# Expert items one by one in a hybrid decoder step: gate/up ahead of the down product, and four weight buffers for all

## The chip, the cores and the metric

The kernel runs on one core of a Trainium2 chip. Its time is the device time of one execution in microseconds (us). TensorE is the matrix engine, VectorE, ScalarE and GpSimd are the others, and SyncE (SP) issues most of the DMAs. A DMA of any queue runs on the core's 16 DMA engines.

## What is computed

The reference is one inference step of a two-layer decoder trunk for 256 prompt rows and 32 sample rows (288 rows of 1024 floats). Layer one mixes rows by a chunked spatial gate, layer two by block-sparse attention. Behind each mixer stands the part that matters here, a mixture of 16 experts: every row picks one of four groups, and in it two of four experts.

```python
g_w, g_idx = lax.top_k(g_prob, 1)
e_w, e_idx = lax.top_k(e_prob, TOP_K_IN_GROUP)          # 2 of the 4 experts in the group
e_w = e_w / jnp.sum(e_w, axis=-1, keepdims=True) * g_w
expert = g_idx * EXPERTS_PER_GROUP + e_idx
gates = jnp.sum(jax.nn.one_hot(expert, N_EXPERTS) * e_w[..., None], axis=1)
a = jnp.einsum('nd,edf->nef', x, w_gate)                # 1024 -> 256 per expert
b = jnp.einsum('nd,edf->nef', x, w_up)
hid = jax.nn.silu(a) * b * gates[:, :, None]
y = jnp.einsum('nef,efd->nd', hid, w_down)              # 256 -> 1024
```

## The kernel before

The kernel doesn't compute every expert for every row. It makes a list of items: one item is one expert with up to 64 of its rows (64 slots, each row in two halves of 512, so 128 partitions). Items 0 to 15 are experts 0 to 15; an expert with more than 64 rows gets extra items behind them. Items are done in pairs, so `plan` writes the number of pairs, and a layer does 16, 18 or more items.

For each item these steps follow one another, each on its engine:

- VectorE makes a one-hot matrix of slots against rows (`one_hot`, L827), TensorE multiplies it with `marks` into a table (`table_of`, L1153), and VectorE turns the table into row indices, output indices and gates (`indices`, L845 to L854). One table serves a pair. Its results move through three stages (`shift`, L834 and L835).
- GpSimd copies the row index (`take`, L501) and issues an indirect DMA that gathers the item's rows from `h_rows` in HBM (L505).
- TensorE transposes the gathered rows (`rows_up`, L1162), and VectorE copies them to `x_slotsT` (`x_tile`, L875).
- TensorE does the gate and up products (L1182), 32 instructions, ScalarE the SiLU (L609), VectorE the product with up and gate (L895).
- TensorE transposes the hidden rows (L1193), VectorE copies them (L899), TensorE does the down product (L1200), 8 instructions, ScalarE copies it out (L612), and GpSimd scatters it to `y_rows` (L531).

In TensorE's queue the order for item q is: gate/up(q), the table of a later pair if q is even, `rows_up` of q+1, the hidden transposes of q, down(q). Nothing of q+1 but its transposes stands between gate/up(q) and down(q).

The weights of an item are 1 MB each for gate, up and down. There are four places for them: `ew_in`/`ew_down` 0 and 1, and `pre_in`/`pre_down` 0 and 1 in `half_a` and `half_b`. Items 0 to 3 are loaded before the layer's experts begin. SP's loop (`experts`, L378) then loads items 4 to 7 to the same places, each gate and up when gate/up of four items earlier is done, its down when that item's down is done; items 8 and up all go to `ew` 0 and 1 and wait for the item two before. SP's queue runs in order, waits included. After the last item SP waits for all scatters and loads the rows back (L411).

The line `hold` only waits; `AHEAD` are offsets of semaphores, so that a loop's waits are on positive values.

Of the kernel before, what the change touches and what calls it, by code (L numbers as in the profile page):

```python
# [27 lines left out]
def const_columns(T, TSA, TS):  # L28

    at, out = 0, {}  # L30
    for name, n in (("ident", P), ("keep_upper", P), ("causal_neg", P), ("cos", T), ("sin", T),
                    ("rotate", ROT), ("own_causal", TSA), ("own_neg", TSA * TSA // (GRP * TS)),
                    ("earlier", 16), ("later", 16), ("spread", TSA), ("before", P), ("limits", 4),
                    ("expert_tri", 256), ("expert_slot", 16), ("extra_slot", 16), ("extra_items", 10),
                    ("evens", 5), ("first_items", 16), ("lanes", 2 * P), ("halves", 2), ("marks", 18)):
        out[name] = slice(at, at + n)
        at += n
    return out, at
# [15 lines left out]
def hybrid_step(nc, t, o):  # L54
# [29 lines left out]
    with ExitStack() as ctx:  # L84
# [3 lines left out]
        def sem(name):  # L88
            return ctx.enter_context(nc.semaphore(name))
# [89 lines left out]
        marks = sb("marks", [P, NT, 2, 6], BF16)  # L179
        lanes = sb("lanes", [P, 2 * P], BF16)  # L180
        late = tri[0:1, 0:10 * NE].rearrange("p (i e) -> p i e", i=10)
        late_n = sb("late_n", [1, 10])
        pairs_f = sb("pairs_f", [1, 8])
        items = sb("items", [1, NE + 10], I32)
        pairs = sb("pairs", [1, 1], I32)
        table = sb("table", [P, 2, 6])
        tok_off = sb("tok_off", [P, 4])
        row_idx = sb("row_idx", [P, 2], I32)

        outs = sb("outs", [P, 3, 2], I32)  # L190
        slot_gates = sb("slot_gates", [P, 3, 2])
        out_idx = [sb(f"out_idx{u}", [P, 1], I32) for u in range(2)]
        in_idx = [sb(f"in_idx{u}", [P, 1], I32) for u in range(2)]
# [34 lines left out]
        hot = z_flat[:, 3712:3712 + 6 * P].bitcast(BF16).rearrange("p (c k n) -> p c k n", c=NT, k=2)  # L228
# [47 lines left out]
        E = [{n: sem(f"e{l}_{n}") for n in """step this slid taken planned xt xt_sb gu silued hid ht ht_sb dn y_sb hot tab idx out  # L276
              in0 in1 w0 w1 wd0 wd1 sc0 sc1""".split()} for l in range(DEPTH)]

        AHEAD = {"xt_sb": 2, "hid": 2, "ht_sb": 2, "y_sb": 2}
        s_pre = [sem(f"s_pre{u}") for u in range(2)]  # L280
        s_yb = [sem(f"s_yb{c}") for c in range(NT)]
# [5 lines left out]
        ISTEPS = 4  # L287
        Y_ORDER = [KT - 1] + list(range(KT - 1))
        QUADS = 2
# [31 lines left out]

        def upto(eng, s, n):

            if n > 0:
                eng.wait_ge(s, n)
# [5 lines left out]
        def _(sp):  # L331
# [41 lines left out]
            def prefetch(l, u):  # L373

                expert_in(l, 2 + u, pre_in[u], s_pre[u])
                expert_down(l, 2 + u, pre_down[u], s_pre[u])

            def experts(l):  # L378


                with sp.Fori(1, QUADS) as i:
                    for u in range(4):

                        w_in, w_down = (ew_in, ew_down) if u < 2 else (pre_in, pre_down)
                        hold(E[l]["gu"], 4 * i - 3 + u)
                        expert_in(l, 4 * i + u, w_in[u % 2], E[l][f"w{u}"] if u < 2 else s_pre[u % 2])
                        hold(E[l]["dn"], 4 * i - 3 + u)
                        expert_down(l, 4 * i + u, w_down[u % 2], E[l][f"wd{u}"] if u < 2 else s_pre[u % 2])

                def item(e, u, before):  # L390

                    hold(E[l]["gu"], before + 1)
                    expert_in(l, e, ew_in[u], E[l][f"w{u}"])
                    hold(E[l]["dn"], before + 1)
                    expert_down(l, e, ew_down[u], E[l][f"wd{u}"])

                for u in range(2):
                    item(4 * QUADS + u, u, 4 * QUADS - 4 + u)
                sp.wait_ge(E[l]["planned"], 1)
                n = sp.value_load(pairs[0:1, 0:1], min_val=NE // 2, max_val=NE // 2 + 5)  # L400
                with sp.Fori(2 * QUADS + 1, n) as i:
                    for u in range(2):
                        e = sp.value_load(items[0:1, bass.ds(2 * i + u, 1)], min_val=0, max_val=NE - 1)
                        item(e, u, 2 * i - 2 + u)
                for u in range(2):
                    hold(E[l][f"sc{u}"], 16 * n + 16)
                    hold(E[l][f"in{u}"], 16 * n + 16)
                hold(E[l]["xt_sb"], AHEAD["xt_sb"] + 2 * n + 1)
# [4 lines left out]
            for u in range(2):  # L413
                expert_in(0, u, ew_in[u], E[0][f"w{u}"])
                expert_down(0, u, ew_down[u], E[0][f"wd{u}"])
# [4 lines left out]
            prefetch(0, 1)  # L420
# [4 lines left out]
            prefetch(0, 0)  # L425
# [33 lines left out]
            prefetch(1, 0)  # L459
            for u in range(2):  # L460
                sp.wait_ge(S["pv"], 7 + u)
                expert_in(1, u, ew_in[u], E[1][f"w{u}"])
                expert_down(1, u, ew_down[u], E[1][f"wd{u}"])
            sp.wait_ge(S["proj"], 2 * KT)
            prefetch(1, 1)
# [12 lines left out]
        def _(pool):  # L478
            for l in range(DEPTH):
                for n, ahead in AHEAD.items():  # L480
                    pool.sem_inc(E[l][n], ahead)
# [6 lines left out]
            pool.tensor_copy(marks[:, :, :, 0:3], cst[:, cols["marks"]].rearrange("p (c k n) -> p c k n", c=NT, k=2)).then_inc(S["fill"], 1)  # L488
            pool.tensor_copy(items[:, 0:NE], cst[0:1, cols["first_items"]]).then_inc(S["fill"], 1)

            def experts(l):
# [7 lines left out]
                def take(u, done):  # L499

                    pool.tensor_copy(in_idx[u][:, :], row_idx[:, u:u + 1]).then_inc(E[l]["taken"], 1)  # L501
                    hold(E[l]["taken"], done)

                def gather(u):
                    pool.indirect_dma_start(out=x_slots[:, u, :], out_offset=None, in_=h_dram.rearrange("t (h n) -> (t h) n", h=2),  # L505
                                            in_offset=bass.IndirectOffsetOnAxis(ap=in_idx[u][:, 0:1], axis=0),
                                            bounds_check=2 * T - 1, oob_is_err=False).then_inc(E[l][f"in{u}"], 16)


# [5 lines left out]
                pool.wait_ge(E[l]["idx"], 1)  # L515
                for u in range(2):
                    take(u, u + 1)
                    gather(u)
                pool.wait_ge(E[l]["planned"], 1)
                n = pool.value_load(pairs[0:1, 0:1], min_val=NE // 2, max_val=NE // 2 + 5)  # L520
                with pool.Fori(0, n) as i:
                    hold(E[l]["idx"], i + 2)
                    for u in range(2):
                        hold(E[l][f"in{u}"], 16 * i + 16)
                        take(u, 2 * i + u + 3)
                        hold(E[l]["xt"], 2 * i + u + 1)
                        gather(u)
                    for u in range(2):
                        hold(E[l]["out"], 2 * i + u + 1)
                        hold(E[l]["y_sb"], AHEAD["y_sb"] + 2 * i + u + 1)  # L530
                        pool.indirect_dma_start(out=y_dram[l].rearrange("t k (h n) -> (t k h) n", h=2),  # L531
                                                out_offset=bass.IndirectOffsetOnAxis(ap=out_idx[u][:, 0:1], axis=0),
                                                in_=y_slots[:, u, :], in_offset=None,
# [1011 lines left out]
```

## Time and profile before

| | us |
|---|---|
| median of 3 runs (range) | 773.92 (772.51 to 776.78) |
| the profiled execution | 770.98 |
| its span, first to last instruction | 769.1 |
| TensorE busy (share of the span) | 628.2 (82%) |
| VectorE busy | 289.6 (38%) |
| ScalarE busy | 157.2 (20%) |
| GpSimd busy | 104.0 (14%) |
| mean granted TensorE clock | 0.914 |
| experts, layer one, first gate/up to end of last down | 186.05 to 311.36 |
| experts, layer two | 602.75 to 744.19 |

The two expert stretches are 267 us of the span. A busy share is a mean over stages with different limits; what an item costs is read from its stretch. Times in a timeline are from the span's start; "idle before" in brackets is how long the engine stood still ahead of the group and what it waited for. PE is TensorE, DVE VectorE, ACT ScalarE, POOL GpSimd.

### The profile page before, as it was taken

To read this page: it belongs to the slowest core of one execution; us is meant where nothing else is said; L and a number is where in the kernel's file an instruction comes from. 1 tells how busy PE (TensorE), PEld (TensorE's weight loads), DVE (VectorE), ACT (ScalarE), POOL (GpSimd) and SP (SyncE) were. 2 spreads that over 40 slices of the span, in tenths; PEclk is the share of its full clock that TensorE was granted. 3 is DMA by queue.
4 is the path that set the end of the run, shared out by engine and by line. 5 is a ranking of instruction groups with operands and counts; after the bars stand their busy time and mean duration, and the time that the engine had idled before them with its cause. 6 is when DMAs were issued, how large, how long until landed. Compare 5 with 4: busy or idle time off the path is not lost.

```text
span 769.1 us, 11977 instructions
## 1 busy us (share of the span) xinstructions
PE 628.2 (82%) x4067; PEld 430.0 (56%) x4067; DVE 289.6 (38%) x889; ACT 157.2 (20%) x326; POOL 104.0 (14%) x155
## 2 busy tenths in 40 slices
PE   5899999964899899279999997973987789898860
PEld 3677767732555555157667674662765456564430
DVE  2202121166334322244666775510027443334314
ACT  2115100020212221121112453211013113121210
POOL 0000000002222322000112000000000323322222
PEclk9999968995999999779999998995999799999995
DMA  9965030051997898599522774779923399699934
GB/s 343 290 266 219 22 150 1 0 212 37 381 410 296 330 412 354 173 386 319 170 95 95 237 245 144 244 222 360 404 80 148 131 401 411 239 406 414 409 138 174
DMA packets 65373, 187.82 MB, mean 244 GB/s; under 512 B 12044, under 2 KB 12606, under 8 KB 60982
## 3 DMA queue, kind: packets, MB, share of 16 engines
q1 hardware_dynamic: 58934, 175.50, 61.2%
q0 software_dynamic: 6400, 11.82, 4.2%
q8 instruction: 23, 0.38, 0.2%
q14 instruction: 16, 0.13, 0.1%
HBM read 182.95 MB, written 13.76 MB: 256 GB/s over the span
## 4 chain that ended last, share of the span: by engine, by line
PE 66%; DMA 10%; DVE 10%; SPq 5%; issue 5%; ACT 2%; DVEq 0%; POOLq 0%
PE PS L1097 26%; PE PS L1182 15%; PE PS L1200 7%; DMA ew_in<-in_moe_w_up 5%; PE PS L1088 3%; SPq L313 2%; SPq L311 2%; PE PS L1311 2%; DMA zT<-y_rows 2%; DMA half_b<-in_b_w_o 2%; PE PS L1268 2%; PE PS L1153 1%; PE PS L1113 1%; DVE zT L895 1%; PE PS L1265 1%
## 5 line engine op out<-in xcount | busy, mean ns | idle before, releaser
L1097 PE MATMUL PS<-hT,half_b 128*128 128x288 f32 x384 | 100.6, 422 | 10.4 <-DMA half_b<-in_b_w_o 7.1
L1182 PE MATMUL PS<-ew_in,zT 128*64 128x256 f32 x832 | 99.3, 392 | 6.3 <-DMA ew_in<-in_moe_w_up 3.1
L1097 PEld LDWEIGHTS PS<-hT,half_b 128*128 128x128 f32 x384 | 75.3, 197 | 34.4 <-issue 11.7
L1182 PEld LDWEIGHTS PS<-ew_in,zT 128*64 128x64 f32 x832 | 68.0, 142 | 45.3 <-issue 26.1
L895 DVE SCALAR_TENSOR_TENSOR zT<-PS,slot_gates,zT 64x256 f32<-64x256 f32 x34 | 16.5, 485 | 146.7 <-ACT zT L609 139.2
L1097 PE MATMUL PS<-hT,half_a 128*128 128x288 f32 x256 | 66.2, 417 | 3.1 <-DVE hT L725 3.1
L1200 PE MATMUL PS<-ew_down,zT 128*64 128x512 f32 x208 | 51.3, 611 | 14.5 <-issue 14.5
L1097 PEld LDWEIGHTS PS<-hT,half_a 128*128 128x128 f32 x256 | 49.0, 194 | 20.0 <-issue 4.1
L531 POOL DMA_INDIRECT y_rows<-zT,out_idx x34 | 34.3, 1010 | 149.4 <-ACT zT L612 149.4
L505 POOL DMA_INDIRECT zT<-h_rows,in_idx x38 | 39.8, 1046 | 50.3 <-PE PS L1162 18.7
L612 ACT COPY zT<-PS 128x512 f32<-128x512 f32 x34 | 19.9, 585 | 128.2 <-PE PS L1200 128.2
L511 POOL DMA_DIRECT2D h_rows<-tokbuf x2 | 1.7, 868 | 323.1 <-ACT tokbuf L600 323.1
L584 ACT ACTIVATE sq<-xT 128x288 f32<-128x288 f32 x32 | 13.6, 442 | 123.2 <-DVE xT L732 95.6
L578 ACT ACT_TABLE_LOAD x25 | 32.1, 1283 | 24.8 <-DVE pairs L867 23.7
L732 DVE TENSOR_TENSOR xT<-PS,xT 128x288 f32<-128x288 f32 x16 | 7.3, 458 | 70.5 <-PE PS L1097 70.5
L1097 PE MATMUL PS<-zT,half_a 128*128 128x288 f32 x128 | 33.4, 420 | 0.0
L1200 PEld LDWEIGHTS PS<-ew_down,zT 128*64 128x64 f32 x208 | 15.0, 137 | 30.7 <-issue 30.7
L723 DVE RECIPROCAL rec<-std 128x288 f32<-128x288 f32 x5 | 9.8, 1953 | 55.7 <-ACT std L588 55.7
L1162 PE MATMUL PS<-cst,zT 128*128 128x128 f32 x144 | 27.7, 316 | 3.1 <-DMA zT<-h_rows,in_idx 3.1
L609 ACT ACTIVATE zT<-PS 64x256 f32<-64x256 f32 x34 | 12.8, 377 | 83.1 <-PE PS L1182 83.1
L1097 PEld LDWEIGHTS PS<-zT,half_a 128*128 128x128 f32 x128 | 25.2, 198 | 7.2
L875 DVE COPY zT<-PS 128x512 f32<-128x512 f32 x36 | 24.9, 692 | 9.4 <-PE PS L1162 5.6
(258 smaller groups left out, 847.3 us busy)
## 6 DMA issues: line engine op xcount, KB each, us to landing
ew_in<-in_moe_w_gate SPq DMA_DIRECT2D x26, 1024.0 KB
ew_in<-in_moe_w_up SPq DMA_DIRECT2D x26, 1024.0 KB
ew_down<-in_moe_w_down SPq DMA_DIRECT2D x26, 1024.0 KB
ew_in<-in_cache_k SPq DMA_DIRECT2D x24, 256.0 KB, 4.8
ew_in<-in_cache_v SPq DMA_DIRECT2D x24, 256.0 KB, 3.4
half_a<-in_a_w_in SPq DMA_DIRECT2D x1, 4096.0 KB, 15.5
half_b<-in_a_w_in SPq DMA_DIRECT2D x1, 4096.0 KB, 25.8
half_a<-in_a_w_out SPq DMA_DIRECT2D x1, 4096.0 KB, 13.8
```

The source lines that it names most:

```text
L311: at = [eng.value_load(pages[0:1, bass.ds(b * NPAGE + j, 1)], min_val=0, max_val=NPOOL - 1) for j in pp]
L505: pool.indirect_dma_start(out=x_slots[:, u, :], out_offset=None, in_=h_dram.rearrange("t (h n) -> (t h) n", h=2), in_offset=bass.IndirectO ...
L531: pool.indirect_dma_start(out=y_dram[l].rearrange("t k (h n) -> (t k h) n", h=2), out_offset=bass.IndirectOffsetOnAxis(ap=out_idx[u][:, 0: ...
L578: act.activation(spare[:, :], eps[:, :], func)
L612: act.copy(y_slots[:, u, :], PS[:, 5 + u, :]).then_inc(E[l]["y_sb"], 1)
L875: dve.tensor_copy(x_slotsT[:, u], PS[:, u, :].rearrange("p (j h n) -> p j h n", j=4, h=2)).then_inc(el["xt_sb"], 1)
L895: dve.scalar_tensor_tensor(out=hid, in0=PS[SLOT:2 * SLOT, 2 + u, 0:EF], scalar=slot_gates[0:SLOT, 0, u:u + 1], in1=silu, op0=ALU.mult, op1 ...
L1088: mm = pe.matmul(PS[:, 7, 0:T], mean_d[:, :], sq[:, k, :], start=(k == 0), stop=(k == KT - 1))
L1097: mm = pe.matmul(PS[:, bank, 0:T], w[:, k, col:col + P], src[:, k, :], start=(k == 0), stop=(k == KT - 1))
L1162: mm = pe.transpose(PS[:, u, j * P:(j + 1) * P], x_slots[:, u, bass.ds(j, P, 4)], ident)
L1182: mm = pe.matmul(PS[f * SLOT:(f + 1) * SLOT, 2 + u, 0:EF], x_slotsT[:, u, k % 4, k // 4, :], w_in[u][:, f, k, :], start=(k == 0), stop=(k ...
L1200: mm = pe.matmul(PS[half * SLOT:(half + 1) * SLOT, 5 + u, :], hidT[:, f, :], w_down[u][:, f, half * HALF:(half + 1) * HALF], start=(f == 0 ...
```

## The change

- **Single items.** Items 0 to 14 are written out one by one, and item 15 and all extra items run in a loop. `plan` writes `n_more`, 1 + the number of extra items, in place of the number of pairs.
- **Order on TensorE.** For item q: gate/up(q), hidden transposes of q-1, table of q+3, `rows_up` of q+1, down(q-1). In the loop the order is gate/up(q), table of q+1, hidden transposes of q, `rows_up` of q+1, down(q).
- **Weights.** Items 0 to 14 all go round the four places, in the order `ew` 0, `pre` 1, `pre` 0, `ew` 1, and wait for the item four before. The down weights of `pre` have a semaphore of their own. Item 15 and the extra items all go to `ew` 1; an extra item's load waits for the item before it (`holds`).
- **Tables.** A table is for one item: 64 slots, each twice, 128 wide (`lanes`). `marks` has nine columns, three groups of three, so that one `tensor_reduce` over each group gives the row index, the output index and the gate (`found`), and one addition of `halves` gives both indices as integers (`where`). They lie in rings of 8; `shift`, `take` and the copies to `out_idx` are gone. The gather reads its index from the ring.
- In the loop VectorE makes the table of item q+1 ahead of the product of item q, and at the end of each turn waits for the scatter of item q (`sc1`) before it moves ring place 0 to place 7.

```diff
+            def expert(l, q, wait):
+                u = (0, 1, 0, 1)[q % 4]
+                streamed = q % 4 in (0, 3)
+                if wait:
+                    sp.wait_ge(E[l]["gu"], q - 3)
+                expert_in(l, q, (ew_in if streamed else pre_in)[u], E[l][f"w{u}"] if streamed else s_pre[u])
+                if wait:
+                    sp.wait_ge(E[l]["dn"], q - 3)
+                expert_down(l, q, (ew_down if streamed else pre_down)[u], E[l][f"wd{u}"] if streamed else s_pre_down[u])
             def experts(l):
+                for q in range(4, LAST):
+                    expert(l, q, True)
                 sp.wait_ge(E[l]["planned"], 1)
+                more = sp.value_load(n_more[0:1, 0:1], min_val=1, max_val=11)
+                with sp.Fori(0, more) as i:
+                    q = i + LAST
+                    e = sp.value_load(items[0:1, bass.ds(q, 1)], min_val=0, max_val=NE - 1)
+                    free = sp.value_load(holds[0:1, bass.ds(i, 1)], min_val=12, max_val=N_MAX - 1)
+                    hold(E[l]["gu"], free)
+                    expert_in(l, e, ew_in[1], E[l]["w1"])
+                    hold(E[l]["dn"], free)
+                    expert_down(l, e, ew_down[1], E[l]["wd1"])
...
+                for q in range(2):
+                    pool.wait_ge(E[l]["idx"], 2 * q + 2)
+                    gather(q, q, q)
+                for q in range(LAST):
+                    if q + 2 <= LAST:
+                        pool.wait_ge(E[l]["idx"], 2 * q + 6)
+                        pool.wait_ge(E[l]["xt"], q + 1)
+                        gather(q + 2, (q + 2) % RING, q % 2)
+                    if q >= 1:
+                        pool.wait_ge(E[l]["y_sb"], q)
+                        scatter(q - 1, (q - 1) % RING, (q - 1) % 2)
+                pool.wait_ge(E[l]["y_sb"], LAST)
+                scatter(LAST - 1, (LAST - 1) % RING, (LAST - 1) % 2)
                 pool.wait_ge(E[l]["planned"], 1)
+                more = pool.value_load(n_more[0:1, 0:1], min_val=1, max_val=11)
+                with pool.Fori(0, more) as i:
+                    q = i + LAST
+                    hold(E[l]["idx"], 2 * q + 4)
+                    hold(E[l]["xt"], q + 1)
+                    gather(q + 1, 0, 1)
+                    hold(E[l]["y_sb"], q + 1)
+                    scatter(q, LAST % RING, 1)
...
+                ready_for(ACT.Silu)
+                for q in range(LAST):
+                    gate(q)
+                    if q >= 1:
+                        out_rows(q - 1, scattered(q - 3)[1])
+                out_rows(LAST - 1, scattered(LAST - 3)[1])
+                more = act.value_load(n_more[0:1, 0:1], min_val=1, max_val=11)
+                with act.Fori(0, more) as i:
+                    q = i + LAST
+                    gate(q)
+                    out_rows(q, 16 * i + scattered(LAST - 2)[1])
...
+            def one_hot(l, q):
                 for c, (_, m) in enumerate(tok):
                     for k in range(2):
+                        last = dve.tensor_scalar(hot[0:m, c, k, :], lanes[0:m, :], slots[0:m, c, k:k + 1],
+                                                 -float(SLOT * q) if isinstance(q, int) else 0.0, ALU.subtract, ALU.is_equal)
                 last.then_inc(E[l]["hot"], 1)
+            def indices(l, q, r):
+                dve.wait_ge(E[l]["tab"], q + 1)
+                dve.tensor_reduce(found[:, r, :], PS[:, 7, 0:9].rearrange("p (a b) -> p a b", a=3), AX.X, ALU.add).then_inc(E[l]["idx"], 1)
+                dve.wait_ge(E[l]["idx"], 2 * q + 1)
+                dve.tensor_tensor(where[:, r, :], found[:, r, 0:2], halves, ALU.add).then_inc(E[l]["idx"], 1)
...
+                one_hot(l, 0)
+                for q in range(3):
+                    indices(l, q, q)
+                    one_hot(l, q + 1)
                 plan(l)
...
+                x_tile(0, 0)
+                for q in range(LAST):
+                    if q >= 1:
+                        gated_up(q - 1)
+                    gated(q, q % RING)
+                    x_tile(q + 1, q)
+                    if q + 3 <= LAST:
+                        if q >= 5:
+                            s, value = scattered(q - 5)
+                            dve.wait_ge(el[s], value)
+                        indices(l, q + 3, (q + 3) % RING)
+                        if q + 4 <= LAST:
+                            one_hot(l, q + 4)
+                gated_up(LAST - 1)
+                dve.tensor_scalar(slots[:, :, :], slots[:, :, :], -float(SLOT * NE), None, ALU.add).then_inc(el["slid"], 1)
+                dve.wait_ge(el["sc0"], scattered(8)[1])
+                more = dve.value_load(n_more[0:1, 0:1], min_val=1, max_val=11)
+                with dve.Fori(0, more) as i:
+                    q = i + LAST
+                    dve.wait_ge(el["slid"], i + 1)
+                    one_hot(l, q + 1)
+                    dve.wait_ge(el["hot"], q + 2)
+                    dve.tensor_scalar(slots[:, :, :], slots[:, :, :], -float(SLOT), None, ALU.add).then_inc(el["slid"], 1)
+                    indices(l, q + 1, 0)
+                    gated(q, LAST % RING)
+                    gated_up(q)
+                    x_tile(q + 1, q + 1)
+                    dve.wait_ge(el["sc1"], more_scattered(i))
+                    dve.wait_ge(el["idx"], 2 * q + 4)
+                    dve.tensor_copy(found[:, LAST % RING, :], found[:, 0, :])
+                    dve.tensor_copy(where[:, LAST % RING, :], where[:, 0, :]).then_inc(el["moved"], 1)
+                    dve.wait_ge(el["moved"], i + 1)
...
+                for q in range(3):
+                    table_of(q)
+                rows_up(0, gathered(0)[1], 0)
+                for q in range(LAST):
+                    gate_up(q, *tiles_in(q), q - 1)
+                    if q >= 1:
+                        gated_up(q - 1)
+                    if q + 3 <= LAST:
+                        table_of(q + 3)
+                    rows_up(q + 1, gathered(q + 1)[1], q)
+                    if q >= 1:
+                        down(q - 1, *tiles_down(q - 1), q - 2)
+                gated_up(LAST - 1)
+                down(LAST - 1, *tiles_down(LAST - 1), LAST - 2)
                 pe.wait_ge(el["planned"], 1)
+                more = pe.value_load(n_more[0:1, 0:1], min_val=1, max_val=11)
+                with pe.Fori(0, more) as i:
+                    q = i + LAST
+                    gate_up(q, ew_in[1], (el["w1"], 32 * i + 32 * (NE // 4)), q)
+                    table_of(q + 1)
+                    gated_up(q)
+                    rows_up(q + 1, 16 * i + gathered(LAST + 2)[1], q + 1)
+                    down(q, ew_down[1], (el["wd1"], 16 * i + 16 * (NE // 4)), q)
```

The lines taken out are those of the functions printed above.

## Rows read from the trace of the kernel before

**Rows 1.** The page, chain that ended last, shares by engine.

```profile
PE 66%; DMA 10%; DVE 10%; SPq 5%; issue 5%; ACT 2%; DVEq 0%; POOLq 0%
```

**Rows 2.** Timeline of PE, first items of layer one.

```profile
186.05 5.47 PE L1182 MATMUL PS<-ew_in,zT 128*64 128x256 f32 x32 [1.38 <-DVE zT L875]
...
195.60 3.65 PE L1182 MATMUL PS<-ew_in,zT 128*64 128x256 f32 x32
...
199.19 0.75 PE L1162 MATMUL PS<-cst,zT 128*128 128x128 f32 x4
...
200.33 0.42 PE L1193 MATMUL PS<-cst,zT 64*128 64x64 f32 x2 [0.40 <-DVE zT L895]
...
201.21 1.94 PE L1200 MATMUL PS<-ew_down,zT 128*64 128x512 f32 x8 [0.46 <-issue]
...
202.95 3.65 PE L1182 MATMUL PS<-half_a,zT 128*64 128x256 f32 x32
...
206.53 0.71 PE L1153 MATMUL PS<-marks,zT 128*128 128x6 bf16 x12
```

**Rows 3.** The same timeline, last down of layer one; item 0 and last down of layer two.

```profile
309.42 1.94 PE L1200 MATMUL PS<-ew_down,zT 128*64 128x512 f32 x8 [0.45 <-issue]
...
602.75 5.33 PE L1182 MATMUL PS<-ew_in,zT 128*64 128x256 f32 x32 [1.65 <-DVE zT L875]
...
742.24 1.94 PE L1200 MATMUL PS<-ew_down,zT 128*64 128x512 f32 x8 [0.46 <-issue]
```

**Rows 4.** Waits in layer two: who waited for whom, total us, times, longest.

```profile
ACT zT L612 <- PE PS L1200: 67.3, 18, 4.0
```

**Rows 5.** DMA queues of two stretches, 200 to 240 and 676 to 732 us: packets, MB, share.

```profile
q1 hardware_dynamic: 3277, 14.88, 92.6%
...
q1 hardware_dynamic: 4635, 21.33, 94.6%
```

**Rows 6.** Windows: busy time of each engine, granted clock, DMA share, GB/s.

```profile
244.00:246.00 2.00, 1.47 (x10) 0.87 (x6) 1.14 (x3) 0.38 (x1) 0.00 (x0) 1.00 0.36 135
...
252.00:254.00 2.00, 1.37 (x12) 1.07 (x13) 1.43 (x4) 0.10 (x1) 1.23 (x2) 1.00 0.46 80
...
660.00:662.00 2.00, 1.61 (x14) 0.89 (x11) 0.58 (x2) 0.38 (x1) 0.09 (x1) 1.00 0.73 297
...
670.00:672.00 2.00, 1.41 (x8) 0.67 (x10) 0.55 (x3) 0.00 (x0) 1.03 (x1) 1.00 0.86 317
```

**Rows 7.** Timeline of SP's queue, issue of item 10's first load.

```profile
251.94 0.41 SPq L333 DMA_DIRECT2D ew_in<-in_moe_w_gate  x1
```

**Rows 8.** The chain, in order of time: start, us, what.

```profile
282.76 12.90 DMA ew_in<-in_moe_w_up
...
699.93 12.23 DMA ew_in<-in_moe_w_up
```

**Rows 9.** Timeline of all engines ahead of item 0, layer one.

```profile
176.16 1.25 DVE L827 TENSOR_SCALAR zT<-lanes,slots 128x256 bf16<-128x256 bf16 x6
...
178.66 0.23 DVE L850 TENSOR_SCALAR row_idx<-tok_off,cst 128x2 int32<-128x2 f32 x1
...
180.22 1.11 POOL L505 DMA_INDIRECT zT<-h_rows,in_idx  x1 [0.96 <-POOL in_idx L501]
...
183.54 1.13 PE L1162 MATMUL PS<-cst,zT 128*128 128x128 f32 x4 [1.80 <-DMA zT<-h_rows,in_idx]
...
185.22 0.69 DVE L875 COPY zT<-PS 128x512 f32<-128x512 f32 x1 [0.95 <-PE PS L1162]
```

**Rows 10.** Landing times of the scatters of L531.

```profile
DMA to landing us min/median/max: 2.3/6.5/7.0
```

**Rows 11.** Timeline of PE in the attention.

```profile
470.02 1.11 PE L1311 MATMUL PS<-cst,half_a 128*128 128x128 f32 x4 [2.54 <-DVE half_a L970]
```

**Rows 12.** Windows around two gaps of PE (PEclk is the granted clock).

```profile
470.00:475.00 5.00, 3.95 (x16) 1.63 (x16) 1.17 (x4) 2.69 (x10) 0.00 (x0) 0.50 0.16 63
...
711.00:713.00 2.00, 0.50 (x6) 0.34 (x6) 1.54 (x9) 1.87 (x3) 0.43 (x1) 1.00 1.03 426
```

More of the change, by code:

```diff
@@ L411, in experts @@
                         load(dst[0:m, c, :], y_dram[l][at:at + m, k, :], s_yb[c])
[L413 to L415 removed]
+            expert(0, 0, False)
+            expert(0, 3, False)
             sp.wait_ge(S["z"], KT)
@@ L458, in _ @@
             sp.wait_ge(S["pv"], 6)
[L459 to L463, printed above, removed]
+            expert(1, 2, False)
+            sp.wait_ge(S["pv"], 7)
+            expert(1, 0, False)
+            sp.wait_ge(S["pv"], 8)
+            expert(1, 3, False)
             sp.wait_ge(S["proj"], 2 * KT)
-            prefetch(1, 1)
+            expert(1, 1, False)
             experts(1)
@@ L514, in experts @@
                     pool.wait_ge(E[l][f"sc{u}"], 16)
[L515 to L518, printed above, removed]
-                pool.wait_ge(E[l]["planned"], 1)
[L520 to L533, printed above, removed]
-                                                bounds_check=4 * T - 1, oob_is_err=False).then_inc(E[l][f"sc{u}"], 16)
@@ L1215, in experts, with gate_up @@
-                with pe.Fori(2 * QUADS, pairs_n) as i:
-                    pair(i, *streamed(i + 1 - QUADS))
+                def gate_up(q, w_in, landed_in, free):
+                    u = u_of(q)
+                    pe.wait_ge(*landed_in)
+                    pe.wait_ge(el["xt_sb"], q + 1)
+                    upto(pe, el["hid"], free)
+                    for k in range(KT):
+                        for f in range(2):
+                            mm = pe.matmul(PS[f * SLOT:(f + 1) * SLOT, 2 + u, 0:EF], x_slotsT[:, u, k % 4, k // 4, :],
+                                           w_in[:, f, k, :], start=(k == 0), stop=(k == KT - 1))
+                    mm.then_inc(el["gu"], 1)
@@ new lines, in gated_up, with down @@
+                def gated_up(q):
+                    pe.wait_ge(el["hid"], q + 1)
+                    upto(pe, el["ht_sb"], q)
+                    if not isinstance(q, int):
+                        pe.sem_inc(S["held"], 1)
+                    for f in range(FB):
+                        mm = pe.transpose(PS[:, 4, f * SLOT:(f + 1) * SLOT], hid[:, bass.ds(f, P, FB)], ident[0:SLOT, 0:SLOT])
+                    mm.then_inc(el["ht"], 1)
+                def down(q, w_down, landed_down, free):
+                    u = u_of(q)
+                    pe.wait_ge(*landed_down)
+                    pe.wait_ge(el["ht_sb"], q + 1)
+                    upto(pe, el["y_sb"], free)
+                    for f in range(FB):
+                        for half in range(2):
+                            mm = pe.matmul(PS[half * SLOT:(half + 1) * SLOT, 5 + u, :], hidT[:, f, :],
+                                           w_down[:, f, half * HALF:(half + 1) * HALF], start=(f == 0), stop=(f == FB - 1))
+                    mm.then_inc(el["dn"], 1)
```

288 lines of the change are left out of this document (103 added, 185 removed).

## The prediction

> **What bounds the kernel now.** I read the chain that ended last first, for which engine carries it: two thirds is TensorE, and a tenth is DMA [rows 1]. Then TensorE's timeline through the expert stretch of each layer, for the time of one item; then the DMA share in short windows, for when the weight stream stands still; last the waits, for how many items there are.
>
> An item on TensorE is gate/up 3.6 us, every second item a table 0.7 (half of it 0.35), the transposes of the next rows 0.7, hidden transposes 0.4, down 1.74 from its start to the next item [rows 2]. From 195.60 to the next item's start at 202.95 it is 7.35 us; with a table 7.7. Of this some 0.4 to 0.65 us twice an item is idle: TensorE waits for SiLU and product (ahead of L1193), then for the copy of the transposes (ahead of L1200). Item 0 starts at 186.05, the last product of the first layer ends at 309.42 + 1.94 = 311.36, of the second at 742.24 + 1.95 = 744.19 [rows 2, 3]. The second layer does 18 items [rows 4]; the two together 34, so the first does 16.
>
> The weight stream is the other limit. In its full stretches the hardware queue moves 14.88 MB in 40 us and 21.33 MB in 56 us [rows 5]: an item of 3.146 MB takes 8.46 or 8.26 us. I take 8.4, which is more than TensorE's 7.5. It is saved by the four items already there and paid back late: the stream stands still from about 244.7 to 253.5 (only 80 GB/s in the window to 254) and, in layer two, from 661.5 to 670 [rows 6], because items 10 and up may use only the two ew buffers (loads of item 10 are issued at 251.94 [rows 7], after item 8's gate/up). From there TensorE waits for weights: item 14's arrive at 295.66 and 712.16 [rows 8].
>
> **The prologue.** Before: one-hot starts 176.16, row index ready 178.89, copied by GpSimd, gather issued 180.22, rows transposed from 183.54, copied at 185.22, item 0 at 186.05 [rows 9]. After: six half-wide compares (0.2 us each as before, 1.05 in all; the trace has 1.25 for 256 wide), half a table 0.4, two VectorE instructions in place of three to reach an index, and no GpSimd copy: index 0 at about 178.0, gather issued about 179.1. But VectorE now makes three indices and four one-hots before item 0's copy: 177.2 + 3 x (0.4 + 0.45 + 1.05) = 182.9, plus a plan shorter by two instructions, 1.15: copy at 184.05, item 0 at 184.95. That is 1.1 us earlier; in layer two, where the first table waits for other transposes, 0.6. If the half-wide compare with two operations costs 0.3 instead of 0.18, this gain is gone (+2.3 us a layer); at its cheapest (0.15) it is 0.6 more.
>
> **Next item's gate/up ahead of the down product.** It adds no instruction: gate/up(q), hidden transposes(q-1), table, rows(q+1), down(q-1). SiLU and product lie under the down product, the copy of the transposes under table and rows, so both idle times go: 3.6 + 0.4 + 0.35 + 0.7 + 1.74 = 6.8 us an item, if VectorE and GpSimd keep up. GpSimd can: the two issues and their preparation are 3.9 us an item. But for the first ten items this gains nothing lasting, since the stream's 8.4 us bounds the end.
>
> **Four buffers for all.** SP's queue runs in order, and behind its wait for down(0) stand the loads of items 5 and on. down(0) comes after gate/up(1), at 184.95 + 5.5 + 0.3 + 0.7 + 1.0 (item 1 waits for its rows' copy here) + 3.6 + 0.4 + 1.0 + 1.94 = 199.4. Item 4's gate and up flow at 192.1 (issue plus 1.5, as around 251.94 [rows 6, 7]) and end at 197.7; the rest flows from 200.9: 3.2 us lost, against 8.8 gained. Then nothing stops it: every slot is free 6.8 us after the last. Item 14's gate/up weights are through 10.0 items later, 284.9. By the same sum item 14 of before would be there at 253.5 + 4.67 x 8.4 = 292.7 and 670 + 39.2 = 709.2; it came 3.0 later both times [rows 8], with other loads under way behind it. So 287.9, and 705.1 in layer two, where item 0 starts at 602.75 - 0.6 [rows 3].
>
> **The tail is where it is given back.** From item 14's weights on, TensorE does gate/up(14) 3.6, hidden(13) 0.4, rows(15) 0.7, down(13) 1.74, hidden(14) 0.4, the now bare copy 0.6, down(14) 1.74 = 9.2: item 15 starts at 297.1 and 714.3 (its own weights are there: 8.4 after item 14's). Reading the count is taken at nothing, under down(14); uncovered it costs 0.95 (the gap on VectorE before the copy at 185.22 [rows 9]).
> Items from 15 on are in the loop, where the table of item q+1 is made after gate/up(q), and the transposes of the rows of q+1 stand ahead of down(q) in TensorE's queue. So each such item holds a whole round trip: table 0.35, index 0.45, gather issued 0.95 later, landing 3.1 after the issue (180.22 to 183.54 [rows 9] is 3.3 at most), transposes 0.7, down 1.94: 7.5 us from the end of gate/up to the end of down, against 3.9 now. The layer ends at 297.1 + 3.65 + 7.5 = 308.2 with the clock held.
> Layer two has one extra item or two by its 18. I routed the given inputs by the reference: its fullest expert has 68 rows, one over 64, so one extra item, and 17 in place of 18. The saved empty item is worth its 7.5 us, but item 16 is serial: its weights wait for gate/up(15) (718.0), flow 719.5, arrive 724.7 to 725.5; and VectorE waits at the loop's end until the scatter of item 15 has landed before it makes the next one-hot. From down(15) (725.5): copy 0.6, scatter 0.9, landing 3.3 (2.3 at the least and 6.5 in the median [rows 10]; item 16's down weights flow just then), moves 0.5, one-hot 1.1, table 0.4, index 0.45, gather 1.1 + 3.0, transposes 0.7, down 1.94 = 14.0: end 739.5.
>
> **The clock.** TensorE idles about 3 us in each such round trip. Idle for 2.54 us ahead of 470.02 [rows 11], its granted clock was 0.50 from 470 to 475; around a gap of 1.5 us, 711 to 713, it stayed 1.00 [rows 12]. So I let it fall from 2.4 to 1.2 GHz after each: +1.5 us on down(15) in both layers, +2.0 on the last transposes and down. The Trainium skill, "TensorE: Matmul & The Clock Gate", Part 1, says that a gate halves the clock after an idle window; by it the rival below in which the clock holds is excluded, where the rows leave it open.
>
> **The sum.** Layer one 309.7 against 311.36: -1.6. Layer two 725.5 + 1.5 + 14.0 + 2.0 = 743.0 against 744.2: -1.2. Together -2.8 us on the profiled 770.98 (span 769.1); the median of the runs shown is 773.92, so 771.1.
>
> **Rivals.**
> *The clock holds* (the gaps are split by small transposes, as that of 1.5 us was): -1.6 - 1.5 and -1.2 - 3.5, together -7.8: 766.1. Against it stands the 470 row. Chance 0.25.
> *The stream gains more*: without the 3.0 us of late landing (less is queued at the end than now) both layers start item 15 up to 2.2 earlier: -2.8 - 4.4 = -7.2, 766.7. Against it: two rows show 3.0. Chance 0.13.
> *Slower: gathers and scatters land late.* If in the loop they take the 6.5 us of [rows 10] in place of 3.0 to 3.3, layer one pays 3.5, layer two 3.5 + 3.2 + 3.5: +13.7, so 784.8. It decides from 1.7 us more a trip (four trips, over 2.8 + 3.9). For it: stray loads behind; against it: the stream is nearly empty in all four. With half of it 778. Chance 0.2.
> The Trainium skill, "DMA: Bandwidth & Descriptors", section "Latency and other measured facts", gives 0.2 us for an HBM access on average and 2 us at high load; by it the four trips would cost at most 7.2 us more, an estimate of 775.6 with everything else as forecast.
> *It doesn't do what it says:* in the static part GpSimd issues gather(q+3) only after scatter(q-1), 3.5 us after down(q-1); landing may take 7.7 before TensorE waits. If it does, the item is 7.5 as now, still under 8.4: nothing changes but the first ten items. It is in the forecast's range.
>
> Forecast (clock falls, landings short) 0.42, its own range 768 to 775. The 80% range takes in the fast rivals (766) with the cheap bound of the compares and item 15 early (762), and half the slow landing: 762 to 779. Within 0.5% (3.9 us, about what this kernel's measurement can tell from no change) are most of the forecast and a little of the slow one, 0.38; faster the two fast rivals, 0.38; slower 0.24, the slow rival and the dear compares.
>
> **What would show it.** Right: DMA share 1.0 from about 201 to 297 with no gap; item 15's gate/up at 297 and 714; 7 to 9 us from its end to the end of down; 33 items; a granted clock of 0.5 in the round trips. Wrong: TensorE idle ahead of the row transposes in items 1 to 14 for more than 1.6 us an item, a stream that pauses again, or round trips of 10 us and more.

## The result and the profile after

The changed kernel takes 780.1 us (median of 4 runs, 779.1 to 782.5), the kernel before beside it 773.2 (772.3 to 776.8): a ratio of 1.008, 95% interval 1.005 to 1.011. It is slower by 0.8%; 771.1 was predicted. The profiled execution took 779.1, its span is 777.1 against 769.1, and its mean granted clock 0.89 against 0.914.

The page of the changed kernel: the chain that ended last, by engine, and the row transposes among its lines (L1194), which answer to [rows 1].

```profile
PE 64%; DMA 19%; DVE 9%; SPq 3%; issue 2%; ACT 2%; POOLq 0%; DVEq 0%; ACTq 0%
...
L1194 PE MATMUL PS<-cst,zT 128*128 128x128 f32 x140 | 28.1, 327 | 11.6 <-DMA zT<-h_rows,where 11.6
```

The share of DMA in the chain has doubled, and TensorE is idle for 11.6 us ahead of the transposes of gathered rows. The timeline of TensorE (start, duration, what, in brackets the idle time ahead of it and what ended it) through layer one, in answer to [rows 2, 3]:

```profile
184.52 6.13 PE L1205 MATMUL PS<-ew_in,zT 128*64 128x256 f32 x32 [1.18 <-DVE zT L885]
...
197.52 1.94 PE L1227 MATMUL PS<-ew_down,zT 128*64 128x512 f32 x8
199.28 3.62 PE L1205 MATMUL PS<-half_a,zT 128*64 128x256 f32 x32
...
205.99 3.62 PE L1205 MATMUL PS<-ew_in,zT 128*64 128x256 f32 x32
...
247.10 3.67 PE L1205 MATMUL PS<-half_b,zT 128*64 128x256 f32 x32 [0.75 <-DMA half_b<-in_moe_w_up]
...
290.11 3.67 PE L1205 MATMUL PS<-half_a,zT 128*64 128x256 f32 x32 [2.04 <-DMA half_a<-in_moe_w_up]
...
299.26 3.65 PE L1205 MATMUL PS<-ew_in,zT 128*64 128x256 f32 x32
302.84 0.39 PE L1184 MATMUL PS<-marks,zT 128*128 128x9 bf16 x6
304.30 0.42 PE L1216 MATMUL PS<-cst,zT 64*128 64x64 f32 x2 [1.07 <-DVE zT L890]
306.92 1.13 PE L1194 MATMUL PS<-cst,zT 128*128 128x128 f32 x4 [2.20 <-DMA zT<-h_rows,where]
307.98 3.68 PE L1227 MATMUL PS<-ew_down,zT 128*64 128x512 f32 x8
```

The period of an item is 6.7 us (199.28 to 205.99) until its weights are late, from item 9 on; then every gate/up up to item 14's waits for them. Items 9 to 14 start 8.60 us apart ((290.11 - 247.10) / 5). The last down product stands behind rows that nobody needs, runs at half clock (3.68 in place of 1.94) and ends at 311.66, where it ended at 311.36 before. What the stream had gained is gone within the last 9 us of the layer.

The same timeline at the end of layer two, from item 15's gate/up, with the instructions of other engines that its waits name:

```profile
719.42 3.67 PE L1205 MATMUL PS<-ew_in,zT 128*64 128x256 f32 x32
...
723.36 0.38 SPq L351 DMA_DIRECT2D ew_in<-in_moe_w_gate  x1
...
723.84 0.42 SPq L351 DMA_DIRECT2D ew_in<-in_moe_w_up  x1
...
724.87 1.04 POOL L508 DMA_INDIRECT zT<-h_rows,where  x1 [2.89 <-issue]
...
730.85 1.13 PE L1194 MATMUL PS<-cst,zT 128*128 128x128 f32 x4 [5.95 <-DMA zT<-h_rows,where]
731.91 3.68 PE L1227 MATMUL PS<-ew_down,zT 128*64 128x512 f32 x8
735.37 3.77 PE L1205 MATMUL PS<-ew_in,zT 128*64 128x256 f32 x32
...
741.01 0.17 DVE L932 COPY found<-found 128x3 f32<-128x3 f32 x1 [8.30 <-DMA y_rows<-zT,where]
...
742.88 0.41 PE L1184 MATMUL PS<-marks,zT 128*128 128x9 bf16 x6 [3.74 <-DVE zT L855]
...
747.97 3.68 PE L1227 MATMUL PS<-ew_down,zT 128*64 128x512 f32 x8
```

SP issues 2 MB of weights for item 16 at 723.36 and 723.84; the gather of item 16's rows is issued 1 us later and reaches TensorE at 730.85. Item 15's down product, whose operands have been there since 725.2, waits behind it. Layer two's experts end at 751.65; from the first gate/up (604.40) they take 147.3 us, 141.4 before. The waits from 600 us on (total, times, longest) count 17 items, so 33 with layer one's 16:

```profile
ACT zT L628 <- PE PS L1227: 66.0, 17, 12.1
```

Of the 8.0 us of span, 0.3 is layer one's end, 1.4 the attention and dense part between the layers, 5.8 layer two's experts, 0.5 what follows them.

### The profile page after: what moved, and what is told of

The parts are those of the page before. It is cut to its first block, busy times and chain, and to the rows that moved or that the text cites. A ratio compares the mean times of both kernels' runs of the same rounds, so it can differ in the third digit from the quotient of the medians.

```text
span 777.1 us, 10893 instructions
## 1 busy us (share of the span) xinstructions
PE 628.2 (81%) x3979; PEld 417.1 (54%) x3979; DVE 277.4 (36%) x794; ACT 134.1 (17%) x294; POOL 92.1 (12%) x114
## 4 chain that ended last, share of the span: by engine, by line
PE 64%; DMA 19%; DVE 9%; SPq 3%; issue 2%; ACT 2%; POOLq 0%; DVEq 0%; ACTq 0%
PE PS L1128 25%; DMA half_a<-in_moe_w_up 12%; PE PS L1205 10%; PE PS L1227 6%; PE PS L1360 3%; PE PS L1119 3%; PE PS L1194 2%; DMA zT<-y_rows 2%; DMA half_b<-in_b_w_o 2%; SPq L351 2%; PE PS L1317 2%; PE PS L1377 2%; PE PS L1144 1%; DMA zT<-h_rows,where 1%; PE PS L1184 1%
## 5 line engine op out<-in xcount | busy, mean ns | idle before, releaser
L1128 PEld LDWEIGHTS PS<-hT,half_b 128*128 128x128 f32 x384 | 75.5, 198 | 34.3 <-issue 11.6
L1205 PE MATMUL PS<-ew_in,zT 128*64 128x256 f32 x544 | 67.0, 402 | 9.2 <-DMA ew_in<-in_moe_w_up 6.3
L1205 PEld LDWEIGHTS PS<-ew_in,zT 128*64 128x64 f32 x544 | 42.2, 146 | 39.2 <-issue 14.1
L896 DVE COPY zT<-PS 128x128 f32<-128x128 f32 x33 | 9.6, 292 | 134.7 <-PE PS L1216 111.9
L513 POOL DMA_INDIRECT y_rows<-zT,where x33 | 33.5, 1014 | 179.0 <-ACT zT L628 174.2
L508 POOL DMA_INDIRECT zT<-h_rows,where x35 | 35.9, 1026 | 59.7 <-DVE where L865 34.2
L1227 PE MATMUL PS<-ew_down,zT 128*64 128x512 f32 x136 | 38.2, 687 | 0.0
L855 DVE TENSOR_SCALAR zT<-lanes,slots 128x128 bf16<-128x128 bf16 (+1 forms) x210 | 37.0, 247 | 1.7 <-DVE slots L917 1.2
L1194 PE MATMUL PS<-cst,zT 128*128 128x128 f32 x140 | 28.1, 327 | 11.6 <-DMA zT<-h_rows,where 11.6
L1205 PE MATMUL PS<-half_a,zT 128*64 128x256 f32 x256 | 29.2, 381 | 9.0 <-DMA half_a<-in_moe_w_up 9.0
L1205 PE MATMUL PS<-half_b,zT 128*64 128x256 f32 x256 | 29.3, 381 | 5.8 <-DMA half_b<-in_moe_w_up 4.0
L1205 PEld LDWEIGHTS PS<-half_a,zT 128*64 128x64 f32 x256 | 18.0, 137 | 22.9 <-DMA half_a<-in_moe_w_up 12.5
```

Source lines behind the costliest of these rows:

```text
L855: last = dve.tensor_scalar(hot[0:m, c, k, :], lanes[0:m, :], slots[0:m, c, k:k + 1], -float(SLOT * q) if isinstance(q, int) else 0.0, ALU. ...
L1128: mm = pe.matmul(PS[:, bank, 0:T], w[:, k, col:col + P], src[:, k, :], start=(k == 0), stop=(k == KT - 1))
L1194: mm = pe.transpose(PS[:, u, j * P:(j + 1) * P], x_slots[:, u, bass.ds(j, P, 4)], ident)
L1205: mm = pe.matmul(PS[f * SLOT:(f + 1) * SLOT, 2 + u, 0:EF], x_slotsT[:, u, k % 4, k // 4, :], w_in[:, f, k, :], start=(k == 0), stop=(k == ...
L1227: mm = pe.matmul(PS[half * SLOT:(half + 1) * SLOT, 5 + u, :], hidT[:, f, :], w_down[:, f, half * HALF:(half + 1) * HALF], start=(f == 0), ...
```

## The experiments

Twelve measurements were made in three groups, each group on one chip with the kernel before: 775.9 us there in the first (19 runs), 773.9 in the second (24), 775.1 in the third (29). Single executions of one kernel lie up to 1.2% apart, so the ratios decide, and differences inside a group.

**Down product ahead of the next rows, in the loop.** TensorE's queue in the loop, both layers:

```
-    rows_up(q + 1, ...)
     down(q, ...)
+    rows_up(q + 1, ...)
```

> The changed kernel with two lines swapped in TensorE's loop for items 15 and up: the down product ahead of the transposes of the next rows. Theory A (the tail's round trip is the loss: the down product stands behind a gather): layer one's last down product ends near 307 us instead of 311.7, layer two's near 741 instead of 751.7, because item 15's down product, its scatter and the copy behind it come 8 us sooner; about 765 to 769 us, faster than the kernel before. Rival B (the tail is bound by the single weight buffer, and the gather only fills that wait): item 16's gate/up starts within 1 us of where it does now, 735.4, and the whole is within 4 us of the changed kernel, 776 to 780.

Measured: 769.3 us (8 runs), 0.992 of the kernel before (0.989 to 0.995). TensorE in layer two:

```profile
725.37 3.62 PE L1227 MATMUL PS<-ew_down,zT 128*64 128x512 f32 x8 [0.43 <-issue]
731.00 0.75 PE L1194 MATMUL PS<-cst,zT 128*128 128x128 f32 x4 [2.01 <-DMA zT<-h_rows,where]
732.60 5.14 PE L1205 MATMUL PS<-ew_in,zT 128*64 128x256 f32 x32 [0.86 <-DVE zT L885]
...
739.99 1.94 PE L1227 MATMUL PS<-ew_down,zT 128*64 128x512 f32 x8 [0.43 <-issue]
```

The rows of item 16 still come at 731.0, but down(15) is done by then and its scatter has nearly landed, so the table of the next item needs no wait (VectorE idles 1.93 us ahead of its moves in place of 8.30). Item 15's gate/up to the last down's end is 22.5 us in place of 32.2. Layer one's last down ends at 307.9. Two lines in another order turn 0.8% slower into 0.8% faster.

**The buffer part alone.** The kernel before, its four buffers used for three turns in place of two:

```
-        QUADS = 2
+        QUADS = 3
```

> The kernel before with one number changed, QUADS from 2 to 3: items 0 to 11 go round four weight buffers instead of 0 to 7, all else as it was. It is the buffer part of the change alone. Theory (the stream's standstill of 8 to 9 us a layer is what makes items 12 and up wait): the standstill moves behind item 13's weights, TensorE no longer waits for weights in layer one, whose last down product ends near 308.5 instead of 311.4, and waits less in layer two; 768 to 771 us, 3 to 5 us faster than before. Rival (the stream's total decides and the standstill only moves): within 1.5 us of before.

Measured: 768.1 us (6 runs), 0.989 (0.985 to 0.992). Layer one's experts end at 308.0 in its profile, and TensorE waits for no weights in either layer. With the second measurement below (767.7 against 773.9), the third turn of the buffers alone is worth 6 to 8 us.

**Item 16's weights only after item 16's rows.** SP's issue is held on the gather:

```
     hold(E[l]["gu"], free)
+    hold(E[l]["in1"], 32 * i + gathered(LAST - 2)[1])
```

> The changed kernel with one more wait in SP's loop: item 16's weights are issued only when the gathered rows of item 16 have landed. It tells why that gather took 5.9 us longer than its partner in layer one. Theory (it queues behind 2 MB of item 16's own weights): TensorE waits about 2.2 us for it instead of 5.95, item 15's down product ends near 732 instead of 735.6, item 16's weights come near 735, so the end hardly moves (within 2 us). Rival (the gather is slow by itself, by its addresses or by the table): the wait stays near 6 us and the whole is 4 us longer.

One execution, 777.3 us. The timeline:

```profile
724.44 1.04 POOL L509 DMA_INDIRECT zT<-h_rows,where  x1 [2.84 <-issue]
...
727.19 1.13 PE L1195 MATMUL PS<-cst,zT 128*128 128x128 f32 x4 [2.72 <-DMA zT<-h_rows,where]
727.38 0.38 SPq L351 DMA_DIRECT2D ew_in<-in_moe_w_gate  x1
...
735.03 1.40 PE L1206 MATMUL PS<-ew_in,zT 128*64 128x256 f32 x8 [3.10 <-DMA ew_in<-in_moe_w_up]
```

With the weights out of the way the rows are there 2.75 us after the gather's issue; behind 2 MB of weights it was 5.98 (724.87 to 730.85). So the gather was late because item 16's weights were under way. Gate/up of item 16 gains nothing (735.03, now waiting 3.1 us for its weights), but item 15's down product and its scatter come earlier, so the last down product still ends sooner, 30.1 us after item 15's start in place of 32.2:

```profile
745.40 3.68 PE L1228 MATMUL PS<-ew_down,zT 128*64 128x512 f32 x8
```

What that is worth in the whole, one execution does not tell.

**The old order for items 0 to 14.** gate/up, table, rows, hidden transposes and down of one item, with VectorE's order to match; the rest of the change stays:

```
-    gate_up(q); gated_up(q - 1); table_of(q + 3); rows_up(q + 1); down(q - 1)
+    gate_up(q); table_of(q + 3); rows_up(q + 1); gated_up(q); down(q)
```

> The changed kernel with items 0 to 14 in the old order on TensorE: gate/up, table, next rows, hidden transposes, down of the same item; VectorE's order follows. Theory A (the weight stream bounds the layer, so running gate/up ahead is worth nothing, and it delays the first down product and with it the stream): items take 7.5 us until the stream catches up, item 4's down weights are issued 3 us sooner, and item 15 starts 1 to 4 us sooner than 299.3; 774 to 780 us. Rival B (running ahead is what keeps TensorE off the path): item 15 starts 3 us or more later, 783 us or more.

Measured: 775.3 us (12 runs), 0.9994 (0.997 to 1.002), although the one profiled execution, at 780.1 its slowest, starts item 15 of layer one at 299.2 as the changed kernel does. By that profile I had read that running ahead is worth nothing. The interval says something else, so it ran again below.

**Down first in one layer.** The edit of the first experiment, in layer one alone, then in layer two alone:

> The changed kernel with down(q) ahead of the transposes of rows(q+1) in layer one alone. In the runs so far layer one's experts ended between 307.9 and 311.7 us, yet the projection that waits for w_o's DMA in the middle started at 535.4 to 537.3 in all but one. Theory (the middle swallows what layer one's experts gain: its projections start earlier but at the lower clock, and then it waits for cache and w_o weights): last down product of layer one ends at 307.9 in place of 311.7, the w_o projection still starts at 536 to 537, and the whole is within 2 us of the changed kernel (778 to 780). Rival (layer one's gain passes through): 3.7 us earlier everywhere behind, 776.

> The same edit in layer two alone. Theory: nearly all of what the edit brought in both layers together (769.3 against 780) comes from here, since nothing behind layer two swallows it: item 15's and item 16's down products no longer stand behind late rows; end of the last down product 7.5 to 9 us earlier than in the changed kernel for the same start, time 770 to 773. Rival (both layers carry equal parts): 775.

> The changed kernel itself, on the same chip as the three beside it, as the base that they are compared with. Theory: 778 to 781, 0.8% over the kernel before. If the 0.8% were a matter of one chip or of how the clock happened to fall, it would be within 0.5% here.

Layer one alone: 776.4 us (12 runs), 1.0027 (1.0005 to 1.0048). Layer two alone: 773.1 (12 runs), 0.9987 (0.9966 to 1.0008). The changed kernel beside them: 779.2 (7 runs), 1.008 (1.005 to 1.011). So by the medians layer one brings 2.8 us and layer two 6.1; by the ratios 4.1 and 7.2, and the intervals allow either. Layer one's experts end 3.5 us earlier than in the first profile of the changed kernel (308.2 against 311.7). My theory that the middle swallows layer one's gain fell: the projection that I expected to start at 536 to 537 started at 534.1, and most of the gain, if not all, comes out at the end.

> The kernel before with QUADS = 3 once more, beside the others: it takes only the third turn of the four buffers and leaves the order of pairs. Theory: 0.988 to 0.992 of the kernel before (765 to 769), level with or a little under the changed kernel with down first in both layers, and clearly under down first in layer two alone, if layer one counts at all; as fast as that one if it does not.

Measured: 767.7 us (6 runs), 0.992 (0.989 to 0.995), as expected.

**Running ahead, measured beside its base.** Four kernels on one chip: the old order again, both edits together, down first alone, the changed kernel.

> The changed kernel with the old order of an item for items 0 to 14, again, now beside the changed kernel on one chip. It had 0.9994 of the kernel before where the changed kernel has 1.008, although in its one profiled execution, its slowest, item 15 of layer one started at the same 299.2 us. Theory (running ahead costs, through the clock or through extra requests that collide, not through the order of the tail): ratio to before 0.998 to 1.002 again, 4 to 7 us under the changed kernel beside it. Rival (the two came from different chips, and running ahead is worth nothing): within 2 us of the changed kernel beside it, 777 to 781.

> Both edits: down(q) ahead of the next rows in the loop, and the old order for items 0 to 14. Theory (running ahead costs 4 to 7 us by itself): 763 to 766, the fastest of all. Rival (worth nothing): the same as down first alone within 2 us, 768 to 770.

> Down first in both layers, as the base of the run with both edits. Both theories: 0.990 to 0.995 of the kernel before, 9 to 12 us under the changed kernel beside it.

> The changed kernel, as the base of the other three on this chip. Both theories: 1.005 to 1.011 of the kernel before.

| | median us (runs) | ratio to before |
|---|---|---|
| the change | 780.1 (12) | 1.0066 (1.004 to 1.009) |
| old order of items | 774.3 (12) | 0.9998 (0.997 to 1.003) |
| down first | 770.0 (12) | 0.9925 (0.990 to 0.995) |
| both | 763.3 (6) | 0.985 (0.981 to 0.989) |

Running ahead costs 5.7 us by itself and 6.7 where down goes first. Both edits together, which keep the four buffers, the single extra items and the short tables, are the fastest version, 1.5% under the kernel before. A part of why it costs shows in SP's queue. First the changed kernel, then the old order (start of item 0: 184.52 and 186.55):

```profile
190.68 0.37 SPq L351 DMA_DIRECT2D ew_in<-in_moe_w_gate  x1
191.09 0.47 SPq L351 DMA_DIRECT2D ew_in<-in_moe_w_up  x1
199.49 0.34 SPq L351 DMA_DIRECT2D ew_down<-in_moe_w_down  x1
```

```profile
192.03 0.37 SPq L351 DMA_DIRECT2D ew_in<-in_moe_w_gate  x1
192.44 0.47 SPq L351 DMA_DIRECT2D ew_in<-in_moe_w_up  x1
196.05 0.34 SPq L351 DMA_DIRECT2D ew_down<-in_moe_w_down  x1
```

Item 4's down weights wait for down(0). Run ahead, down(0) stands behind a whole gate/up, and 8.4 us pass between the issues of up and down weights in place of 3.6: the stream has run dry meanwhile (a DMA share of 0.03 from 198 to 200 us, 1.03 in the old order). TensorE's waits in layer two, 600 to 720 us, first of the changed kernel on this chip:

```profile
PE PS L1205 <- DMA half_a<-in_moe_w_up: 4.9, 2, 3.0
PE PS L1205 <- DMA ew_in<-in_moe_w_up: 3.3, 2, 1.7
...
PE PS L1205 <- DMA half_b<-in_moe_w_up: 1.6, 1, 1.6
```

and all those of the old order that are over 1 us:

```profile
PE PS L1225 <- issue: 7.5, 13, 0.6
PE PS L1203 <- DVE zT L885: 1.6, 1, 1.6
PE PS L1182 <- DVE zT L855: 1.5, 1, 1.5
PE PS L1225 <- DVE zT L896: 1.3, 2, 0.6
```

In the old order TensorE waits for no weights at all, although item 14's have to be there only 0.8 us later (711.52 against 710.74). And when the stream does bind, running ahead is the worse place to be caught: from item 14's gate/up to item 15's are 9.28 us (710.74 to 720.02: two down products lie between), in the old order 7.34 (711.52 to 718.86). From the start of layer two's item 0 to item 15's gate/up it is 114.8 us run ahead and 113.6 in the old order; from 116.3 to 113.4 with down first.

So these rows account for 1.2 and 2.9 us in layer two. But about 1.6 of the 2.9 is the clock: in that profile of down first, item 14's gate/up ran at half clock for a part, behind its wait for weights, and item 15's starts 10.83 us after it in place of the 9.28 above:

```profile
706.99 5.36 PE L1205 MATMUL PS<-half_a,zT 128*64 128x256 f32 x32 [1.97 <-DMA half_a<-in_moe_w_up]
```

In six of the eight profiles of kernels that run ahead, one to four gate/up products behind such a wait took 5.36 us in place of 3.67; the three profiles of the old order have no such wait and no such product. So running ahead has a second price, which differs from one execution to the next. How much of it reaches the end is not shown.

In layer one the same stretch is 1.7 shorter (113.0 against 114.7), but item 0 starts 2.0 later there in all three profiles of the old order, since the first gather comes 5.1 us after its issue in place of 3.3; why, stays open. The profiled execution of the old order was, at 778.4, again 4 us over its median, so how the 5.7 us add up in a typical execution stays open too.

## Why the prediction was wrong, by its steps

The forecast of the span was 766.3; it is 777.1. Two steps failed by what they assumed, that running ahead "gains nothing lasting" (put at nothing, measured at 5.7 to 6.7 us lost) and that the stream is nearly empty in every round trip (one trip of 9.0 us took 12.5); the time of the weight stream was mis-sized besides, by 5.0 us in the two layers. The 10.8 us between forecast and profile, step by step:

- **Prologue: right.** Item 0 of layer one starts at 184.52, forecast 184.95. The six half-wide compares take 1.05, and GpSimd copies nothing.
- **6.8 us an item run ahead: right**, 6.7. That it "gains nothing lasting" was the trap: I priced it at nothing for items 0 to 9, and it costs. I had its two prices in the text, the 3.2 us in which the stream stands still at item 4 and the 9.2 from item 14's weights to item 15's start, and compared neither with the old order, where they are nothing and 7.35.
- **Item 14's weights at 287.9 and 705.1: wrong by 2.2 and 5.2.** The item was put at 8.4 us of stream, between 8.46 and 8.26 [rows 5]; it is 8.60 here (above). Ten items at 0.2 are 2.0 us a layer. From item 0's start, items 15 began 2.6 and 2.9 late; with item 0 of layer one 0.4 early, that is 2.2 and 2.9: 5.0 us. What the other 0.6 to 0.9 a layer is, was not followed.
- **Layer one's round trip and fallen clock: right.** Gate/up's end to down's end, 7.5 + 1.5 forecast, is 8.8 (302.9 to 311.66), with the last down at half clock. The windows of the changed kernel show the granted clock of 304 to 310 and 731 to 735, in answer to [rows 12]:

```profile
304.00:310.00 6.00, 3.50 (x12) 1.80 (x14) 1.13 (x3) 0.00 (x0) 1.04 (x1) 0.63 0.02 3
731.00:735.00 4.00, 4.00 (x12) 1.57 (x14) 0.69 (x1) 0.00 (x0) 0.00 (x0) 0.50 0.00 0
```

  The Trainium skill, "TensorE: Matmul & The Clock Gate", Part 1, has the clock halved after idling, and the trace agrees (0.50 in the second window, behind an idle time of 5.95 us). In all three profiles of the changed kernel the down products of the three trips ran at half clock, wholly or in part (2.86 to 3.68 us in place of 1.94). But that the rival in which the clock holds was excluded beforehand, as the prediction has it, goes too far: idle times of 2 us left the clock up in one execution of this kernel and halved it in another (last section).
- **Layer two's trip of item 15: the step that failed is "the stream is nearly empty in all four".** It is not in this one: SP issues item 16's weights on the same event, the end of gate/up(15), that starts the round trip, and 1 us ahead of its gather. The prediction has these weights in its own text ("flow 719.5, arrive 724.7 to 725.5") and did not set them beside the gather. The trip took 12.5 us in place of 9.0: 3.5 more. The rival of late landings had the mechanism and priced it at 3.2 to 3.5 in each of four trips; one had it. The estimate of 775.6 behind that rival is added up wrong (771.1 and 7.2 is 778.3), and it gives a trip 1.8 us more where this gather took 3.2 more (5.98 against 2.75).
- **The extra item: right.** From down(15)'s end to the last down's end, 14.0 + 2.0 forecast, 16.06 measured: the scatter landed 3.9 us after its issue (737.15 to 741.01), the gather came 2.2 after.
- **The middle: not priced, 2.0 us.** The forecast moved layer one's gain through unchanged. In these two profiles TensorE's clock came back later after the change. The mean squares and first projection of layer two, before:

```profile
329.86 5.73 PE L1088 MATMUL PS<-sq,mean_d 128*128 128x288 f32 x16 [0.64 <-ACT sq L584]
338.88 9.69 PE L1097 MATMUL PS<-hT,half_b 128*128 128x288 f32 x32 [3.29 <-DVE hT L725]
```

and after:

```profile
330.11 7.19 PE L1119 MATMUL PS<-sq,mean_d 128*128 128x288 f32 x16 [0.64 <-ACT sq L595]
340.59 10.94 PE L1128 MATMUL PS<-hT,half_b 128*128 128x288 f32 x32 [3.29 <-DVE hT L753]
```

  That is 2.7 us in two groups of instructions that are the same in both kernels. The granted clock was 0.50 from 322 to 333 us in both; from there to 337 it was 0.99 before, and after the change still 0.50 until 335. But nothing shows that the change does this. A second profile of the changed kernel, whose last down product ran at half clock too, has the short times:

```profile
332.45 5.65 PE L1119 MATMUL PS<-sq,mean_d 128*128 128x288 f32 x16 [0.64 <-ACT sq L595]
341.39 9.69 PE L1128 MATMUL PS<-hT,half_b 128*128 128x288 f32 x32 [3.29 <-DVE hT L753]
```

  And the kernel before with three turns of its buffers took the long ones in one profile (7.11 and 10.89), with its last down product at full clock, and the short ones in the other. From the last down of layer one to item 0 of layer two, the changed kernel takes 292.7, 290.3 and 293.5 us in its three profiles, and the kernel before 291.4 in its one. So this term is as large as what it differs by from one execution to the next.
- **After the experts**: 0.5 us more (25.4 against 24.9).

The terms 2.16 + 2.87 + 3.47 + 1.95 + 0.54, less the 0.14 by which layer one's trip and layer two's tail together beat the forecast, are 10.85. Against the kernel before, which is what the ratio measures, the experiments weigh the parts: down behind the next rows +10.1 us (780.1 to 770.0; +11.1 in the old order, 774.3 to 763.3), running ahead +5.7 to +6.7, the rest of the change -11.8 (763.3 against 775.1). Of that rest the third turn of the buffers brings 6 to 8 us by itself; the single items, the short tables and the item saved in layer two were not measured one by one. I had named the transposes "ahead of down(q) in TensorE's queue" and summed their trips, but set them off against gains that mostly came from buffers, and forecast the balance, 2.8 us, from terms of 10.

## What to carry to other kernels

On an in-order engine, work that waits for a long round trip goes behind all that is ready: two lines in the other order were worth 1.3% here (780.1 to 770.0), at the end of the loop where nothing follows to hide the trip. Running ahead delays every release of what the late half holds, so ask what each release starts; here it was a weight buffer, and behind it the whole in-order weight queue. Where a gain and a loss of 10 us are set against each other, measure the parts one by one, since the sign of the whole says nothing about them.

## What the runs showed of the hardware that I had not expected

- A gather issued 1 us after 2 MB of weights came 5.95 us later than the engine was ready for it, and 2.72 with the stream empty; so here the small gather of GpSimd got no precedence over SP's weights.
- An idle time of about 2 us ahead of item 14's gate/up left the clock up in one profile of the changed kernel (layer one, 290.11: 3.67 us behind 2.04 idle) and halved it for a part of the 32 matmuls in another profile of the same kernel:

```profile
290.73 5.36 PE L1205 MATMUL PS<-half_a,zT 128*64 128x256 f32 x32 [2.05 <-DMA half_a<-in_moe_w_up]
```

  The same in layer two, in the changed kernel (3.67 us) and in the second measurement of down first (5.36 us), with 1.96 and 1.97 idle. The windows of 706 to 712 us, of the one and of the other (the seventh value is the granted clock):

```profile
706.00:712.00 6.00, 4.04 (x28) 1.91 (x28) 1.24 (x3) 0.58 (x1) 1.02 (x1) 1.00 1.03 412
```

```profile
706.00:712.00 6.00, 5.01 (x32) 3.01 (x32) 0.00 (x0) 0.00 (x0) 1.02 (x1) 0.72 0.99 402
```

  So the length of a gap alone does not tell whether the clock falls.
- From 201 to 285 us, the stream of layer one moved 31.01 MB in 84 us on SP's queue beside 3.10 MB of gathers and scatters, 407 GB/s together.
